# Moving the merge arithmetic of an attention phase to the end of VectorE's step

## The reference

```python
for g, (window, dilation) in enumerate(DILATION_PATTERNS):
    q = rms_norm(qkv[:, :, 0, g], q_gain[g]) * (ATTN_HEAD_DIM ** -0.5)
    k = rms_norm(qkv[:, :, 1, g], k_gain[g])
    o, l = dilated_window_attention(q, k, qkv[:, :, 2, g], rel_bias[:, g], window, dilation)
    outs.append(o)
    lses.append(l)
wts = jax.nn.softmax(jnp.stack(lses), axis=0)
y = jnp.einsum('gbsh,gbshe->bshe', wts, jnp.stack(outs))
```

## Time and profile before

| | |
|---|---|
| median of 3 runs | 3356.33 us (3354.56 to 3357.91) |
| the profiled execution | 3356.33 us, its span 3354.6 us |
| TensorE (PE) busy | 3188.1 us, 95% of the span |
| VectorE (DVE) busy | 1337.2 us, 40% |
| ScalarE (ACT) busy | 1107.3 us, 33% |
| GpSimd (POOL) busy | 824.2 us, 25% |
| granted TensorE clock, mean | 0.973 |

### The profile page before, as it was taken

The page is one execution under the profiler, slowest core; times in us unless marked ns, Lnnn a source line. Parts: engine busy times, 40 slices in busy tenths (PEclk is TensorE's granted clock), DMA queues, the critical chain, the costliest instruction groups (busy, mean ns, idle before and its releaser), DMA issues. The chain is left out here.

```text
span 3354.6 us, 48256 instructions
## 1 busy us (share of the span) xinstructions
PE 3188.1 (95%) x17466; PEld 2671.8 (80%) x17466; DVE 1337.2 (40%) x3725; ACT 1107.3 (33%) x3002; POOL 824.2 (25%) x598
## 2 busy tenths in 40 slices
PE   4999999999999995999999999899877999999999
PEld 3888888888888884788888888678665788888887
DVE  6446565555546554431313133531064422313131
ACT  4555555555555553210202112111254211111110
POOL 3333333333233311122222222112211212222121
PEclk8999999999999996999999999999898999999999
DMA  2112121121212104111111111111201111111112
GB/s 98 37 38 63 40 61 52 50 56 46 54 44 62 51 16 164 38 51 51 44 51 49 46 51 45 36 47 45 81 32 51 45 50 51 44 51 45 50 49 78
DMA packets 89904, 177.01 MB, mean 53 GB/s; under 512 B 25515, under 2 KB 55870, under 8 KB 89662
## 3 DMA queue, kind: packets, MB, share of 16 engines
q1 hardware_dynamic: 87358, 169.63, 15.9%
q10 hardware_dynamic: 2304, 4.20, 0.3%
HBM read 160.67 MB, written 13.12 MB: 52 GB/s over the span
## 5 line engine op out<-in xcount | busy, mean ns | idle before, releaser
L69 PE MATMUL ps_qk<-w_hi,attn_hT_hi 128*128 128x256 f32 x1536 | 438.1, 285 | 22.7 <-DVE attn_hT_lo L213 9.7
L915 POOL TENSOR_TENSOR first_w_lo<-first_raw,first_w_hi 128x1024 fp32r<-128x1024 f32 x96 | 231.7, 2413 | 901.6 <-ACT first_w_hi L911 901.6
L70 PE MATMUL ps_qk<-w_lo,attn_hT_hi 128*128 128x256 f32 x1536 | 436.7, 284 | 0.0
L71 PE MATMUL ps_qk<-w_hi,attn_hT_lo 128*128 128x256 f32 x1536 | 436.6, 284 | 0.0
L857 POOL TENSOR_TENSOR w_lo<-raw,w_hi 128x384 fp32r<-128x384 f32 x192 | 193.7, 1010 | 660.1 <-ACT w_hi L602 660.1
L915 POOL TENSOR_TENSOR second_w_lo<-second_raw,second_w_hi 128x1024 fp32r<-128x1024 f32 x72 | 172.2, 2392 | 630.1 <-ACT second_w_hi L911 630.1
L69 PEld LDWEIGHTS ps_qk<-w_hi,attn_hT_hi 128*128 128x128 f32 x1536 | 294.8, 192 | 27.0 <-issue 12.7
L70 PEld LDWEIGHTS ps_qk<-w_lo,attn_hT_hi 128*128 128x128 f32 x1536 | 295.6, 192 | 0.4
L71 PEld LDWEIGHTS ps_qk<-w_hi,attn_hT_lo 128*128 128x128 f32 x1536 | 295.7, 193 | 0.0
L69 PE MATMUL first_ps<-first_hid_hi,first_w_hi 128*128 128x512 f32 x640 | 255.6, 399 | 32.4 <-DVE first_hid_lo L1239 32.4
L635 ACT ACTIVATE prob<-ps_s,neg_max 128x128 f32<-128x128 f32 (+1 forms) x384 | 156.3, 412 | 362.3 <-DVE neg_max L726 362.3
(11 more groups left out here) (276 smaller groups left out, 6850.3 us busy)
## 6 DMA issues: line engine op xcount, KB each, us to landing
raw<-in_wqkv SPq DMA_DIRECT2D x192, 192.0 KB, 2.3
first_raw<-in_w SPq DMA_DIRECT2D x64, 512.0 KB, 3.4
second_raw<-in_w SPq DMA_DIRECT2D x64, 512.0 KB, 3.4
w_bc<-share_dram SPq DMA_DIRECT2D x48, 256.0 KB, 4.4
first_raw<-in_vo_pieces SPq DMA_DIRECT2D x16, 512.0 KB, 3.5
bias<-bias_dram SPq DMA_DIRECT2D x16, 256.0 KB, 3.5
yT_dram<-o_g SPq DMA_DIRECT2D x8, 512.0 KB, 3.2
first_raw<-in_attn_wo SPq DMA_DIRECT2D x8, 512.0 KB, 3.5
```

What stands on the lines that cost most here:

```text
L69: pe.matmul(out, a_hi, b_hi, start=first, stop=False)
L70: pe.matmul(out, a_hi, b_lo, start=False, stop=False)
L71: return pe.matmul(out, a_lo, b_hi, start=False, stop=last)
L915: pool.tensor_tensor(self.lo[:, n % 2, :], self.raw[:, n % self.RAW, :], self.hi[:, n % 2, :].bitcast(F32), ALU.subtract).then_inc(self.lo ...
```

## The change

The call of `merge_step` in VectorE's step moves from the place behind `neg_max` to the last place of the step, behind `qkn`. Nothing else changes: the same instructions with the same waits are issued.

```diff
@@ -725,7 +725,6 @@
                     dve.wait_ge(maxed, 2 * U)
                     dve.tensor_scalar(neg_max[:, sp_, u:2 * TT:TT], stat[:, sp_, u:2 * TT:TT], -1.0, None,
                                       ALU.mult).then_inc(neg_done, 1)
-                merge_step(i, st, j)
                 if st < SECTIONS:
                     dve.wait_ge(squared, T + 1)
                     if TT * st + j >= 1:
@@ -781,6 +780,7 @@
                                       ps_qk[j % 2][:, 0:2 * P].rearrange("p (h e) -> p h e", e=HD),
                                       rs[:].rearrange("p (h o) -> p h o", o=1).to_broadcast([P, 4, HD]), ALU.mult)\
                         .then_inc(qkn_done, 1)
+                merge_step(i, st, j)
 
             def merge_step(i, st, j):
 
```

## The result

The changed kernel takes 3385.97 us (median of 4 runs, 3383.95 to 3388.28), the kernel before 3357.12 us beside it. The ratio is 1.0089, 95% interval 1.0077 to 1.0101: slower, by 28.9 us. Forecast were 3388 us, 31.7 us more than before. The profiled execution has a span of 3382.0 us, 27.4 us longer than before.

A forecast was written before the change was run, and what follows sets the result against it. TensorE alone was taken to bound supersteps 1 to 23 (1131.90 of 1139 us busy). Place costs of 0.51 + 0.96 + 1.30 + 1.77 = 4.54 us a pair, seven pairs, 31.8 us, added to 3356.33 give 3388 us; range 3371 to 3404 us.

The forecast's parts named there:

- Nothing to gain in the old place: Behind `neg_max`, merge work fits VectorE's 2.70 us wait for `sq`; taking it out gives nothing.
- The cost of each place: Per pair: nine small operations 0.51 us, L830 0.96, L837 1.30, L844 1.77; L794, five small operations, L840, L847 cost 0.
- The direct way: From ScalarE's exponentials straight to TensorE's `ps_p`: 1.30 us of room in a wide step, so not the way that decides.
- The carry of 0.65 us into L844: Some 0.65 us of lateness stay after L840's narrow step, so L844 delays j = 4 by 2.61 us, costing 1.77 us.
- Seven pairs alike: Each of seven pairs loses 4.54 us while TensorE projects, 31.8 us in all.
- Where TensorE waits: New idle before `ps_p` in j = 2, 4 (1.0, 1.4 us), a little in j = 5; before `ps_o` in j = 0 (1 us).
- Queues: SyncE's first transfer had 8.6 us of cover after the nine small operations; some 3 us remain.
- The clock: TensorE's clock stays at 1.00, since the expected stalls are 0.5 to 1.8 us and rarer than in the mLSTM cell.
- Only the direct way: Rival: only lateness from exponentials to `ps_p` counts, 1.62 us a pair, 11 us in all, 3368 us; chance 0.10.
- No change: Rival: the bias is not next in need, VectorE having 2.70 us to spare in each step; 3356 us, chance 0.07.
- Faster: Rival: `qkn` comes up to 2 us earlier in steps with merge work; 3354.5 us, down to 3349 us, chance 0.03.
- The clock falls too: Rival: TensorE's clock also drops after stalls, 12 or 48 us more, 3400 or 3436 us; chance 0.08.

The follow-up runs named there:

- early dose: Kernel before, plus one unread VectorE sum over 1792 elements (2.01 us) behind `neg_max` in every step of supersteps 1 to 23; 3360.3 us.
- two written-out runs: Kernel before and changed kernel, each with supersteps 4 to 21 written out instead of looped; 3346.9 us and 3374.1 us.
- longer late dose: Kernel before, plus one unread VectorE sum over 1536 elements (1.74 us) behind `qkn` in every step of supersteps 1 to 23; 3529.3 us.
- first half late: Kernel before, with only the merge work of supersteps 3p+4 moved behind `qkn`; ratio 1.0024.
- shorter dose: Kernel before, plus one unread VectorE sum over 768 elements (0.94 us) behind `qkn` in every step of supersteps 1 to 23; 3397.8 us.
- second half late: Kernel before, with only the merge work of supersteps 3p+5 moved behind `qkn`; ratio 1.0056.
- weights last: Changed kernel, with ScalarE's copy of the next section's weights moved to the end of its step and GpSimd's `w_lo` following; ratio 1.0073.

## Why the prediction was right, point by point

**Nothing to gain in the old place.** Right: no step got shorter but the one at the first turn of the loop, where the clock decides. The early dose shows that the hole before `ss` holds 2 us, together with the merge work, in all steps of a pair but two, which lose 0.15 and 0.35 us (j = 4 and 5 of superstep 3p+5). The hole was forecast as 2.7 us in all wide steps; behind late merge work it is 2.5 us.

**The cost of each place.** Right to 0.1 us in the table above, for pairs 0 to 5: the threshold of 1.09 us of a wide step, the 0.20 us of j = 0, the 0.66 us of j = 2. L794, the five small operations, L840 and L847 cost nothing by themselves, as forecast. The direct way has less room than the 1.30 us that I took from a wide step of group 0: in j = 2 of superstep 3p+5 it is 0.89 us and in j = 4 1.17 us. It doesn't change the sum, since the way through `sq` and `pT_lo` ends last there too.

**The carry of 0.65 us into L844.** Right: 1.08 us alone, 1.69 us with it, and L844 starts 0.63 us later against `ps_p`.

**Seven pairs alike.** This step failed, by 1.9 us. I multiplied by seven, but superstep 23 is the last section: ScalarE has no weights of a next section to copy there, so 0.5 us more room before `sq`, and GpSimd none either. Pair 6 costs 2.56 and not 4.54 us. The two written-out runs leave the loop 0.2 us of that. That ScalarE's copy makes the rest is borne out by the steps: in superstep 23 `ps_o` no longer waits for `pT_lo` in j = 2 and 4, no lateness is carried into L844 (it starts 2.56 us after `ps_p`), and what stays is the direct way, 0.96 and 0.76 us. With the copy moved in all steps the same holds for all pairs, once the overlap with `w_lo` is taken off. The other six pairs came out 0.1 us cheaper each than forecast.

**Where TensorE waits.** Mostly right. The waits for `prob` in j = 2 and 4 are shown as 0.90 and 1.25 us, and `ps_p` starts 1.06 and 1.43 us later (1.0 and 1.4 us forecast). In j = 0 TensorE waits not before `ps_o`, as I wrote, but before the scores just ahead of it (0.72 us), which at j = 0 need `v_lo`; it is the same lateness, one instruction earlier. In j = 5 of superstep 3p+4 there is no wait of a size that the table shows; the loss is 0.25 us at `ps_p` and 0.22 us at `ps_o`.

**Queues.** Right: SyncE's first transfer starts 4.65 us after the end of the nine operations (587.66 and 583.01), 8.6 us before; some 3 us were forecast. For pair 6 it starts at once, in both kernels. While TensorE projects no product waits for `w_bc`.

**The clock.** Right for the new stalls: 14 waits of up to 1.25 us left it at 1.00. Not foreseen were the pauses that both kernels have, behind which it falls in one execution and not in the next: 2 us of the difference between the profiled spans, in the changed kernel's favour. The rule of the Trainium skill that I had set against the mLSTM row ("TensorE: Matmul & The Clock Gate", "A second HAM failure mode: psum-queue depth-cycling") was not borne out for stalls of this size; the longer late dose, with a wait for `prob` in most steps, still has 0.99, and the rest is lost at the two turns of the loop.

**The rivals.** "Only the direct way" (3368 us) is out by the first half late, whose places cost 8.9 us, of which `ps_p` directly behind the exponentials takes 0.25 us a pair. But this way was put too low: with its true rooms it makes 2.7 of the 4.4 us of a pair, and the way through `pT_lo` adds to it. "No change" is out by the doses. "Faster" is out. "The clock falls too" is out for the stalls of this change.

**Open.** The 0.36 us in superstep 24 (the written-out kernel without the change has them too, so they are not the merge work's), the 1.15 us of the shorter dose around j = 0, the 0.2 us a pair that the loop adds, and why the pauses at the loop's turns differ between runs.

## What to carry to other kernels

An engine with half its time idle is not free everywhere: ask where in its order the idle time lies, and what waits behind the place in which the work is put. Here the same work costs nothing ahead of a wait of 2.7 us and up to 1.7 us a place ahead of the first link of a chain that runs through three engines. The room of a place can be added up from the idle times shown on the links of the chain, less the hand-over; what exceeds it stops the bound engine, and what the chain does not recover is charged to the next place. Where two ways lead to the bound engine, work out both; the one that is later counts. Check such a sum for the first and last rounds of a loop separately, since engines have other work there.

## What the runs showed of the hardware that was not expected

- Behind a pause of TensorE of 2.5 us or more the clock mostly falls to half, but not always. In the nine profiled kernels with a loop it fell at 16 of the 18 turns and stayed at 1.00 at two, with pauses of 2.74 and 2.99 us, while it fell behind one of 2.52 us. In the kernel before a fall costs 1.7 us (0.76 over 7 us). How much of the scatter between runs of one kernel comes from this no run shows.
- A hardware loop costs TensorE at least 2.5 us at each of its two turns, here 8.7 us with the clock. Most pauses were 2.5 to 3.1 us; the run with the second half late had one of 4.4 us, that with the weights last 4.1 us, and those with a late dose 3.7 to 5.8 us. 18 supersteps written out cost nothing that could be seen.
- VectorE's two-input operations wait for GpSimd's `w_lo` where they overlap it, and the wait is shown as a longer duration and not as idle time (2.50 against 2.02 us for L844, 0.45 against 0.17 us for a small one).
